# Transposes one merge step later, and w_down copied to bf16 in DRAM during the first merge, in a hybrid decoder layer on eight cores

## The chip, the cores and the metric

The kernel runs on all 8 cores of one Trainium2 chip. Each core computes 4 of the 32 sequences; the cores share no data. The metric is the device time of the slowest core in microseconds (us).

## The reference

One decoder layer on x of 32 sequences, 2048 tokens, 1024 channels, in float32. Two token mixers (A: sliding-window attention with sinks; B: compressed, selected and windowed attention) give `oa` and `ob`. What follows them is what the change touches:

```python
y = gm[:, :, 0] * (oa @ w_proj_a) + gm[:, :, 1] * (ob @ w_proj_b)   # gm = sigmoid(x @ w_gm)
m = y @ w_out
h = layer_norm(ALPHA * x + m, ln1_g, ln1_b)
f = (silu(h @ w_gate) * (h @ w_up)) @ w_down                        # w_down: 2816 x 1024
x = layer_norm(ALPHA * h + f, ln2_g, ln2_b)
```

## The kernel before, in words

Every core goes through its four sequences one after the other (`sequence`): projections (`phase_p`), attention (`attention`), and `phase_cd`, which holds the merge, the gate/up product and the down product. All matmuls are bf16 into float32 PSUM. The weights come as float32. In the first sequence `load` fetches a weight block with a DMA on GpSimd's queue ("pool") that casts it to bf16 into SBUF, and a store on SP's queue writes the bf16 block to a tensor in DRAM (`wg_b`, `wu_b`, `wd_b` and others); four such stores are kept back in a list (`flush_stores(4)`). In the later sequences the same `load` reads the bf16 block from DRAM on SP's queue.

The order of the work is that of the code, written by hand; each engine executes its own instructions in that order, and `Sched` puts semaphore waits in front of an instruction by the buffers it reads and writes.

The merge (`phase_cd`, first loop) goes over 4 token chunks `tc` of 512 tokens and 8 channel blocks `fc` of 128. A block `c1(fc, tc)` is, for each of the two mixers, 8 gate matmuls (`wgm`, L315) and 4 projection matmuls (`Wpa`/`Wpb`, L314) into PSUM banks 0 to 3, a sigmoid on ScalarE (`sg`, L340) that reads bank 0 or 2, a product on VectorE (`tm`), and at the end a sum into `yT`. From the second chunk on, one step of a list `todo` follows each block. The steps handle tiles `t` of 128 tokens:

- `c2_mm(t)`: 16 matmuls with `Wout` (L316) into banks 4 and 5, the residual sum on VectorE (L355), then `ln_front`: statistics on VectorE, a `pow` on GpSimd, one more VectorE operation.
- `c2_norm(t)`: the normalisation on ScalarE (`pre`, L340), and a multiply with `ln1g` on GpSimd.
- `c2_back(t)`: the addition of `ln1b` on VectorE, the cast into `hbf` on ScalarE (L364), the store of `hs` and the load of a new `pre` tile on SP's queue.
- `c2_tr(t)`: 8 transposes of `hbf` on TensorE (L335) into bank 6 or 7, and the copy into `hT` on ScalarE (L364).

24 of the 34 steps stand in the merge; the other ten follow the first ten hidden blocks of the gate/up stage. That stage takes the tokens in two halves. For each of the 22 hidden blocks `hc` it makes 32 matmuls (L317) from `hT` and two ring blocks `ffr` (w_gate, w_up) into banks 0 to 3; a ring of 6 blocks is refilled by `load_ring`, of which four loads are made early, in the merge at `tc == 2`. ScalarE applies Silu (`sgt`, L340), VectorE multiplies (`actf`). In the first half the 22 blocks of `Wd` are loaded too, one at each of the first ten `hc`, two at each of the next six. The down product (L318) follows each half.

Of the kernel before, what the change touches and what calls it, by code (L numbers as in the profile page):

```python
# [6 lines left out]
BF16 = mybir.dt.bfloat16  # L7
# [5 lines left out]
NT = 16  # L13
DH = 64
FFN = 2816
NHC = 22
# [272 lines left out]
class KB:  # L289
# [163 lines left out]
    def load(self, dst, nm, i, b):  # L453

        if nm not in self.wb:
            self.wb[nm] = self.nc.dram_tensor(nm + "_b", list(self.dr[nm].shape), BF16, kind="Internal").ap()
            self.b_wb[nm] = {}

        def part(ap):
            return ap if i is None else ap[:, i, :] if nm == "wd" else ap[i]  # L460

        if any(p[2] is b for p in self.stores):
            self.flush_stores()
        kept = self.b_wb[nm].get(i)
        if kept is not None and kept.w:
            self.s.dma("sp", (dst, part(self.wb[nm])), reads=[kept], writes=[b])
            return
        kept = self.b_wb[nm][i] = Buf(nm)
        self.s.dma("pool", (dst, part(self.dr[nm])), writes=[b])
        self.stores.append((part(self.wb[nm]), dst, b, kept))  # L470
        self.flush_stores(4)

    def flush_stores(self, n=0):
        while len(self.stores) > n:
            out, src, b, kept = self.stores.pop(0)
            self.s.dma("sp", (out, src), reads=[b], writes=[kept])
# [635 lines left out]
    def phase_cd(self, sq):  # L1112
# [36 lines left out]
        def c1(fc, tc):  # L1149
            ts_ = slice(tc * 512, (tc + 1) * 512)  # L1150
            for i in range(2):
                j = self.wgm_at[2 * fc + i]
                for k in range(8):
                    self.mm("c1g", bk[2 * i][:], wgm[:, j, k, :], self.xT[:, k, ts_], k == 0, k == 7,
                            [self.b_wgm[j], b_xT[tc]], [bb[2 * i]])
                Wp = (Wpa, Wpb)[i]
                for k in range(4):
                    self.mm("c1p", bk[2 * i + 1][:], Wp[:, k, fc * 128:(fc + 1) * 128], self.OT[:, 4 * i + k, ts_],
                            k == 0, k == 3, [b_wp[i], self.b_OT[2 * i + k // 2][tc]], [bb[2 * i + 1]])
                self.act(sg[i], bk[2 * i][:], AF.Sigmoid, [bb[2 * i]], [b_sg[i]])  # L1160
                self.tt(tm[i], bk[2 * i + 1][:], sg[i], ALU.mult, [bb[2 * i + 1], b_sg[i]], [b_tm[i]])
            self.tt(yT[tc % 2][:, fc, :], tm[0], tm[1], ALU.add, [b_tm[0], b_tm[1]], [b_yT[tc % 2]])
# [36 lines left out]

        todo = []  # L1200
        for t in range(NT):
            todo.append([(c2_mm, t)] + ([(c2_back, t - 1)] if t else []))
            todo.append([(c2_norm, t)] + ([(c2_tr, t - 1)] if t else []))
        todo += [[(c2_back, NT - 1)], [(c2_tr, NT - 1)]]

        def c2_step():
            for f, t in todo.pop(0):
                f(t)
# [7 lines left out]
        def load_ring(n):  # L1216
            nonlocal nb
            for _ in range(n):
                if nb < len(blocks):
                    nm, hc = blocks[nb]  # L1220
                    self.load(ring[nb % 6][:], nm, hc, b_ring[nb % 6])
                    nb += 1

        for tc in range(4):
            if tc == 2:
                load_ring(4)
            for fc in range(8):
                c1(fc, tc)
                if tc > 0:
                    c2_step()  # L1230
# [21 lines left out]
        for half in range(2):  # L1252
            b_act = [Buf("act%d%d" % (half, i), spans=strided(M_ACT + 1024 * i, 2048, NHC, 1024)) for i in range(2)]
            for hc in range(NHC):
                w = [((half * NHC + hc) * 2 + i) % 6 for i in range(2)]
                load_ring(2)
                for t2 in range(2):
                    tc = 2 * half + t2
# [122 lines left out]
```

How the kernel before makes its waits and increments, by code:

```python
    def _wait(self, e, key, val):  # L89
        if val <= 0:
            return
        if self.seen[e].get(key, 0) >= val:
            return
        self.eng[e].wait_ge(self.sem[key], val)
        self.seen[e][key] = val
# [31 lines left out]
    def op(self, e, fn, reads=(), writes=(), war=(), parts=128):  # L127
        self._deps(e, reads, writes, war)
        if e == "pool":
            if parts != self.pool_parts or parts == 32:
                self._wait(e, e, self.cnt[e])
            self.pool_parts = parts
        inst = fn()
        self.cnt[e] += 1
        c = self.cnt[e]
        inst.then_inc(self.sem[e], 1)
        for b in reads:
            if b.r.get(e, 0) < c:
                b.r[e] = c
        for b in writes:
            b.w = {e: c}
            b.r = {}
        self.n_inst += 1
        return inst
# [1 line left out]
    def dma(self, q, pairs, reads=(), writes=(), war=()):  # L146
        if not isinstance(pairs, list):
            pairs = [pairs]
        keys = self.dma_keys[q]
        key = keys[self.dma_next[q] % len(keys)]
        self.dma_next[q] += 1
        self._wait(q, key, self.dma_val[key])
        self._deps(q, reads, writes, war)
        for out, in_ in pairs:
            self.eng[q].dma_start(out=out, in_=in_).then_inc(self.sem[key], 16)
        self.dma_val[key] += 16 * len(pairs)
        v = self.dma_val[key]
        for b in reads:
            b.r[key] = v
        for b in writes:
            b.w = {key: v}
            b.r = {}
        self.n_inst += len(pairs)
```

## Time and profile before

| | |
|---|---|
| median of 3 runs | 4913.55 us (4782.35 to 5346.75) |
| the profiled execution: its time | 4829.63 us |
| its span, slowest core (6) | 4828.6 us |
| TensorE (PE) busy | 4343.9 us, 90% of the span |
| VectorE (DVE) busy | 2002.6 us, 41% |
| ScalarE (ACT) busy | 1746.8 us, 36% |
| GpSimd (POOL) busy | 989.6 us, 20% |
| DMA | 438.16 MB, mean 91 GB/s |

Busy time is that of the instructions of one engine; matmuls are pipelined, so a matmul record is longer than the time until the next one may start. The granted clock is TensorE's, as a share of full speed. A wait names the engine and tile that released it. Line numbers are those of the code above; helpers that record an operation (`act` L340, `tt` L344, `stt` L355, `cp` L364, `dma` L156, `tr` L335) give their line to all of their callers, so the tile names tell them apart.

### The profile page before, as it was taken

The page shows a single profiled execution, that of the slowest core. Times are in us where ns is not written, and L with a number is a line of the kernel's source. Part 1 is how long each engine was busy: PE and PEld are TensorE (multiplying, and loading weights), DVE is VectorE, ACT ScalarE, POOL GpSimd, SP SyncE. Part 2 cuts the span into 40 slices and gives each one's busy share as a digit, 9 for nine tenths or more (in the row PEclk, how much of TensorE's full clock was granted, in tenths as well). Part 3 has the DMA queues.
Part 4 walks back from the last instruction along what each step waited for, and adds up shares of the span by engine and source line. Part 5 has one row for each costly group of instructions (what it writes and reads, how often), then busy time and mean ns, then how long its engine had stood idle before and what let it go on. Part 6 is the DMA issues. An engine that isn't in the chain of part 4 may idle for free.

```text
span 4828.6 us, 81987 instructions; the slowest of 8 cores (4763.4 to 4828.6 us)
## 1 busy us (share of the span) xinstructions
PE 4343.9 (90%) x26552; PEld 2127.8 (44%) x27000; DVE 2002.6 (41%) x4784; ACT 1746.8 (36%) x2187; POOL 989.6 (20%) x891
## 2 busy tenths in 40 slices
PE   6868899899987899999998789999998788999998
PEld 3434444344444444444444444444444444444443
DVE  2544454132465445422355444523136544542313
ACT  1368433111237843311125872321122685331111
POOL 4321122120342112101143111202024210210101
PEclk8999999999999999999999999999999999999887
DMA  8340236934232012335333002252432201124130
GB/s 146 125 105 2 56 103 151 230 95 127 82 98 66 2 62 79 121 124 140 83 100 126 2 24 74 71 171 79 148 95 84 90 2 54 70 96 153 66 92 35
DMA packets 225809, 438.16 MB, mean 91 GB/s; under 512 B 26864, under 2 KB 98928, under 8 KB 222192
## 3 DMA queue, kind: packets, MB, share of 16 engines
q1 hardware_dynamic: 189312, 380.01, 23.7%
q0 software_dynamic: 33008, 50.77, 7.2%
q8 instruction: 227, 3.72, 0.3%
q10 hardware_dynamic: 3072, 2.10, 0.2%
q14 instruction: 190, 1.56, 0.1%
HBM read 352.95 MB, written 124.31 MB: 99 GB/s over the span
## 4 chain that ended last, share of the span: by engine, by line
PE 70%; DMA 11%; ACT 8%; DVE 5%; issue 4%; SPq 1%; POOL 1%; DVEq 0%; POOLq 0%; ACTq 0%
PE bpair L317 24%; PE bpair L318 13%; PE bpair L315 8%; ACT pt L340 6%; DMA qd<-ro 5%; PE bpair L316 5%; PE bpair L307 4%; PE bpair L314 4%; PE bpair L302 3%; DMA qd<-zr 2%; PE bpair L308 2%; PE bpair L312 2%; DMA ffr<-wg 1%; PE bpair L335 1%; PE bpair L309 1%
## 5 line engine op out<-in xcount | busy, mean ns | idle before, releaser
L317 PE MATMUL bpair<-hT,ffr 128*128 128x512 bf16 x5512 | 1259.4, 389 | 28.1 <-DMA ffr<-wg 19.3
L340 ACT ACTIVATE pt<-bpair 128x1024 bf16<-128x1024 f32 (+1 forms) x1016 | 990.8, 1019 | 241.0 <-PE bpair L313 114.9
L317 PEld LDWEIGHTS bpair<-hT,ffr 128*128 128x128 bf16 x5632 | 558.4, 100 | 716.0 <-issue 148.8
L318 PE MATMUL bpair<-Wd,actf 128*128 128x512 bf16 x2756 | 635.4, 393 | 3.6
L344 DVE TENSOR_TENSOR actf<-sgt,bpair 128x512 bf16<-128x512 f32 x352 | 240.8, 688 | 950.6 <-PE bpair L317 928.5
L340 ACT ACTIVATE sgt<-bpair 128x512 f32<-128x512 f32 x352 | 207.9, 596 | 867.4 <-PE bpair L317 866.9
L302 PE MATMUL bpair<-xT,w 128*128 128x512 bf16 x1615 | 396.2, 398 | 101.2 <-DVE small L344 59.7
L315 PE MATMUL bpair<-xT,wgm 128*128 128x512 bf16 x1996 | 482.7, 382 | 3.5 <-issue 0.4
L318 PEld LDWEIGHTS bpair<-Wd,actf 128*128 128x128 bf16 x2816 | 282.8, 100 | 355.6 <-issue 100.4
L307 PE MATMUL bpair<-Qr,Ksl 128*128 128x512 bf16 x1088 | 341.6, 384 | 77.7 <-ACT pt L340 48.1
L344 POOL TENSOR_TENSOR sb_lnst<-sb_lnst,sb_mhalf 128x1 f32<-128x1 f32 x128 | 70.3, 549 | 1562.6 <-DVE sb_lnst L350 1562.6
L344 POOL TENSOR_TENSOR ro<-t,t 128x512 bf16<-128x512 f32 (+1 forms) x192 | 241.5, 1275 | 372.2 <-DVE small L344 181.7
L344 DVE TENSOR_TENSOR tm<-bpair,sg 128x512 f32<-128x512 f32 x256 | 172.9, 690 | 322.5 <-PE bpair L314 147.0
L315 PEld LDWEIGHTS bpair<-xT,wgm 128*128 128x128 bf16 x2048 | 198.4, 98 | 236.4 <-issue 6.9
L340 ACT ACTIVATE H<-H,sb_lnst 128x1024 f32<-128x1024 f32 x64 | 79.4, 1241 | 610.3 <-DVE sb_lnst L351 610.3
L302 PEld LDWEIGHTS bpair<-xT,w 128*128 128x128 bf16 x1664 | 163.2, 101 | 297.1 <-issue 136.3
L312 PEld LDWEIGHTS bpair<-V,pt 128*128 128x128 bf16 x4352 | 214.6, 98 | 147.0 <-issue 20.7
L364 ACT CAST hbf<-pre 128x1024 bf16<-128x1024 f32 x64 | 66.8, 1044 | 549.2 <-DVE pre L344 549.2
L312 PE MATMUL bpair<-V,pt 128*128 128x65 bf16 x4352 | 237.2, 195 | 10.9 <-DVE tmpo L344 8.4
L340 ACT ACTIVATE sg<-bpair 128x512 f32<-128x512 f32 x256 | 148.3, 597 | 245.7 <-PE bpair L315 235.0
L316 PE MATMUL bpair<-Wout,yT 128*128 128x512 bf16 x1012 | 230.9, 380 | 0.6
L344 POOL TENSOR_TENSOR pre<-pre,ln1g 128x1024 f32<-128x1024 f32 x64 | 164.4, 2568 | 290.9 <-ACT pre L340 290.9
(131 smaller groups left out, 4520.7 us busy)
## 6 DMA issues: line engine op xcount, KB each, us to landing
ffr<-wg_b SPq DMA_DIRECT2D x154, 256.0 KB, 3.1
ffr<-wu_b SPq DMA_DIRECT2D x154, 256.0 KB, 3.1
pre<-x SPq DMA_DIRECT2D x64, 512.0 KB, 3.5
hs<-pre SPq DMA_DIRECT2D x64, 512.0 KB, 2.6
H<-hs SPq DMA_DIRECT2D x64, 512.0 KB, 3.9
out<-H SPq DMA_DIRECT2D x64, 512.0 KB, 2.6
Wd<-wd_b SPq DMA_DIRECT2D x66, 256.0 KB, 4.4
xT<-xt POOLq DMA_DIRECT2D x16, 1024.0 KB, 15.2
```

What stands on the lines that cost most here:

```text
L302: "fm": lambda *a, **k: t.matmul(*a, **k),
L307: "ss": lambda *a, **k: t.matmul(*a, **k),
L308: "sw": lambda *a, **k: t.matmul(*a, **k),
L312: "pvs": lambda *a, **k: t.matmul(*a, **k),
L314: "c1p": lambda *a, **k: t.matmul(*a, **k),
L315: "c1g": lambda *a, **k: t.matmul(*a, **k),
L316: "c2": lambda *a, **k: t.matmul(*a, **k),
L317: "gu": lambda *a, **k: t.matmul(*a, **k),
L318: "dn": lambda *a, **k: t.matmul(*a, **k),
L340: return self.s.op("act", lambda: nc.scalar.activation(out=out, in_=in_, func=func, **kw), reads, writes, war)
L344: return self.s.op(eng, lambda: e.tensor_tensor(out=out, in0=in0, in1=in1, op=op), reads, writes, war, out.shape[0])
L364: return self.s.op("act", lambda: nc.scalar.copy(out=out, in_=in_), reads, writes, war)
```

## The change

Two edits. In the list of steps the transposes of tile t-2 stand now behind `c2_mm(t)` and `c2_back(t-1)`, where those of tile t-1 stood behind `c2_norm(t)`. And w_down is copied block by block from float32 to bf16 within DRAM, by casting DMAs on GpSimd's queue, one ahead of each of the first 22 blocks `c1` of the first sequence; the loads of `Wd` in the first sequence then find the bf16 block kept and run on SP's queue, as in the later sequences, and their stores fall away.

```diff
+    def copy_wd(self, i):
+
+        if not i:
+            self.wb["wd"] = self.nc.dram_tensor("wd_b", list(self.dr["wd"].shape), BF16, kind="Internal").ap()
+            self.b_wb["wd"] = {}
+        b = self.b_wb["wd"][i] = Buf("wd")
+        self.s.dma("pool", (self.wb["wd"][:, i, :], self.dr["wd"][:, i, :]), writes=[b])
...
         for t in range(NT):
-            todo.append([(c2_mm, t)] + ([(c2_back, t - 1)] if t else []))
-            todo.append([(c2_norm, t)] + ([(c2_tr, t - 1)] if t else []))
-        todo += [[(c2_back, NT - 1)], [(c2_tr, NT - 1)]]
+            todo.append([(c2_mm, t)] + ([(c2_back, t - 1)] if t else []) + ([(c2_tr, t - 2)] if t > 1 else []))
+            todo.append([(c2_norm, t)])
+        todo += [[(c2_back, NT - 1), (c2_tr, NT - 2)], [(c2_tr, NT - 1)]]
...
             for fc in range(8):
+                i = 8 * tc + fc
+                if i < NHC and "wd" not in self.wb or i and len(self.b_wb["wd"]) == i < NHC:
+                    self.copy_wd(i)
                 c1(fc, tc)
```

ScalarE in the first merge, before (`sg` the sigmoids of a block, `pre` the normalisation, `hbf` the cast, `hT` the copy of the transposes):

```order
379 L364 CAST hbf_79_7786<-pre_75_7782 128x1024
380 L340 ACTIVATE sg_68_7775<-bpair 128x512
381 L340 ACTIVATE sg_69_7776<-bpair 128x512
382 L340 ACTIVATE pre_76_7783<-pre_76_7783,sb_lnst 128x1024
383 L364 COPY hT_44<-bpair 128x8x128
384 L340 ACTIVATE sg_68_7775<-bpair 128x512
385 L340 ACTIVATE sg_69_7776<-bpair 128x512
```

The same place after:

```order
378 L364 CAST hbf_79_7786<-pre_75_7782 128x1024
379 L364 COPY hT_44<-bpair 128x8x128
380 L340 ACTIVATE sg_68_7775<-bpair 128x512
381 L340 ACTIVATE sg_69_7776<-bpair 128x512
382 L340 ACTIVATE pre_76_7783<-pre_76_7783,sb_lnst 128x1024
383 L340 ACTIVATE sg_68_7775<-bpair 128x512
384 L340 ACTIVATE sg_69_7776<-bpair 128x512
```

The copy into `hT` has moved from behind the normalisation to directly behind the cast, ahead of the two sigmoids of the next block.

TensorE at the same place, before (`wgm` gate matmuls, `OT,Wpa`/`Wpb` projections, `Wout` those of `c2_mm`, `hbf` the transposes):

```order
1023 L316 MATMUL bpair<-Wout_7746,yT_72_7779 128x512 x16
1024 L315 MATMUL bpair<-xT_43,wgm_2818 128x512 x8
1025 L314 MATMUL bpair<-OT_125,Wpa_2819 128x512 x4
1026 L315 MATMUL bpair<-xT_43,wgm_2818 128x512 x8
1027 L314 MATMUL bpair<-OT_125,Wpb_2820 128x512 x4
1028 L335 MATMUL bpair<-sb_ident,hbf_79_7786 128x128 x8
1029 L315 MATMUL bpair<-xT_43,wgm_2818 128x512 x8
```

and after:

```order
1032 L316 MATMUL bpair<-Wout_7746,yT_72_7779 128x512 x16
1033 L335 MATMUL bpair<-sb_ident,hbf_79_7786 128x128 x8
1034 L315 MATMUL bpair<-xT_43,wgm_2818 128x512 x8
1035 L314 MATMUL bpair<-OT_125,Wpa_2819 128x512 x4
1036 L315 MATMUL bpair<-xT_43,wgm_2818 128x512 x8
1037 L314 MATMUL bpair<-OT_125,Wpb_2820 128x512 x4
1038 L315 MATMUL bpair<-xT_43,wgm_2818 128x512 x8
```

The transposes stand directly behind the 16 matmuls of `c2_mm`, one block earlier in the row than before but for an older tile.

GpSimd in the first sequence's gate/up stage, before (`ffr` the ring, `sb_lnst` the pow, `pre` the multiply):

```order
187 L344 TENSOR_TENSOR sb_lnst<-sb_lnst,sb_mhalf 128x1
188 L156 DMA Wd_9935<-wd 128x1024
189 L156 DMA ffr_82_7797<-wg 128x1024
190 L156 DMA ffr_83_7798<-wu 128x1024
191 L344 TENSOR_TENSOR pre_74_7781<-pre_74_7781,ln1g_7767 128x1024
192 L156 DMA Wd_9935<-wd 128x1024
```

and after, first at the start of the merge, then in that stage:

```order
155 L156 DMA wgm_2818<-wgm 128x1024 x4
156 L156 DMA Wout_7746<-wout 128x8192
157 L156 DMA wd_b<-wd 128x1024 x9
158 L344 TENSOR_TENSOR sb_lnst<-sb_lnst,sb_mhalf 128x1
159 L156 DMA wd_b<-wd 128x1024
...
201 L344 TENSOR_TENSOR sb_lnst<-sb_lnst,sb_mhalf 128x1
202 L156 DMA ffr_82_7797<-wg 128x1024
203 L156 DMA ffr_83_7798<-wu 128x1024
204 L344 TENSOR_TENSOR pre_74_7781<-pre_74_7781,ln1g_7767 128x1024
```

The casting transfers of `wd` have left the stage and stand in the merge, nine of them behind the load of Wout with nothing of GpSimd's between them.

## Rows read from the trace of the kernel before

**Rows 1.** Cores: span, granted clock; then the medians of the dies.
```profile
core 6: 4828.6 us, clock 0.964
...
die 0 (median of its cores): 4765.8 us, clock 0.980
die 1 (median of its cores): 4800.8 us, clock 0.967
```

**Rows 2.** Windows: start:end, length; PE, PEld, DVE, ACT, POOL busy; PEclk, DMA share, GB/s.
```profile
535.00:763.00 228.00, 213.75 (x1019) 97.89 (x1038) 116.20 (x189) 67.94 (x95) 39.76 (x31) 0.99 0.33 93
763.00:964.00 201.00, 178.56 (x800) 78.53 (x817) 50.23 (x79) 44.03 (x64) 47.26 (x71) 0.95 0.98 215
1958.00:2126.00 168.00, 167.16 (x798) 77.49 (x812) 50.22 (x79) 43.61 (x63) 14.23 (x9) 1.00 0.49 159
...
4541.00:4723.00 182.00, 180.80 (x692) 76.06 (x704) 34.50 (x51) 27.39 (x45) 2.90 (x2) 0.83 0.28 87
```

**Rows 3.** Tile ffr, first gate/up stage of two sequences: ns min/median/max, first and last start.
```profile
L317 PEld LDWEIGHTS bpair<-hT,ffr x704: 94/98/153, 763.8 to 963.8; 128*128 128x128 bf16 x176
...
L317 PEld LDWEIGHTS bpair<-hT,ffr x704: 96/98/98, 1958.2 to 2125.8; 128*128 128x128 bf16 x176
```

**Rows 4.** Waits in 763 to 964 us, PE and SP's queue: total, times, longest.
```profile
PE bpair L317 <- DMA ffr<-wg: 19.3, 8, 4.8
...
SPq L94 <- DMA Wd<-wd: 46.6, 18, 4.8
```

**Rows 5.** Waits of PE over the whole span.
```profile
PE bpair L335 <- ACT hbf L364: 53.6, 44, 1.5
```

**Rows 6.** Timeline of one merge cycle, second sequence: start, length, engine, operation, idle.
```profile
1825.83 1.89 PE L315 MATMUL bpair<-xT,wgm 128*128 128x512 bf16 x8
...
1829.88 1.22 DVE L344 TENSOR_TENSOR pre<-pre,ln1b 128x1024 f32<-128x1024 f32 x1
...
1831.19 1.04 ACT L364 CAST hbf<-pre 128x1024 bf16<-128x1024 f32 x1 [8.71 <-DVE pre L344]
1832.14 1.08 ACT L340 ACTIVATE sg<-bpair 128x512 f32<-128x512 f32 x2
...
1832.38 0.61 PE L335 MATMUL bpair<-sb_ident,hbf 128*128 128x128 bf16 x8 [1.20 <-ACT hbf L364]
...
1832.87 1.89 PE L315 MATMUL bpair<-xT,wgm 128*128 128x512 bf16 x8
...
1834.24 1.01 ACT L364 COPY hT<-bpair 128x1024 bf16<-128x1024 bf16 x1
...
1835.13 0.61 ACT L340 ACTIVATE sg<-bpair 128x512 f32<-128x512 f32 x1
...
1838.05 3.19 PE L316 MATMUL bpair<-Wout,yT 128*128 128x512 bf16 x13
```

**Rows 7.** Timeline of a step in the second sequence's gate/up stage.
```profile
1986.35 7.07 PE L317 MATMUL bpair<-hT,ffr 128*128 128x512 bf16 x31
...
1991.71 1.04 ACT L364 CAST hbf<-pre 128x1024 bf16<-128x1024 f32 x1 [9.57 <-DVE pre L344]
...
1992.66 1.08 ACT L340 ACTIVATE sgt<-bpair 128x512 f32<-128x512 f32 x2
...
1993.70 2.54 PE L317 MATMUL bpair<-hT,ffr 128*128 128x512 bf16 x11
```

**Rows 8.** DMA issues: count, KB each, median us to landing; last, GpSimd's issue time in ns.
```profile
ffr<-wg POOLq DMA_DIRECT2D x22, 256.0 KB, 12.9
...
Wd<-wd_b SPq DMA_DIRECT2D x66, 256.0 KB, 4.4
...
Wd<-wd POOLq DMA_DIRECT2D x22, 256.0 KB, 16.1
wd_b<-Wd SPq DMA_DIRECT2D x22, 256.0 KB, 11.7
...
L156 POOL DMA_DIRECT2D Wd<-wd x22: 527/547/591, 778.2 to 911.9; - x22
```

## Prediction

> **What bounds the kernel now.** I read the cores first. Core 6 is the slowest, 4828.6 us at a granted clock of 0.964; the median of die 0 is 4765.8 us at 0.980 [rows 1]. So 62.8 us of the profiled time belong to die 1 alone. The windows show where: in the last gate/up stage of the last sequence the clock stands at 0.83, where the undisturbed stages stand at 0.99 or 1.00 [rows 2]. Nothing in the change touches that, but it tells how far a measured time can lie from the sum.
>
> Second, the same windows say which engine bounds the two stages that the change touches. In the merge of the first sequence TensorE is busy 213.75 of 228 us, while DMA is at a share of 0.33. In the first gate/up stage of the second sequence it is busy 167.16 of 168 us with DMA at 0.49. In the same stage of the first sequence, where the weights still come in as float32 and are written back as bf16, DMA is at 0.98 of all 16 engines over 201 us, and the clock at 0.95 [rows 2]. Third, the tile view of the ring weights gives that stage's length from its first to its last weight load: 200.0 us in the first sequence (763.8 to 963.8), 167.6 us in the second (1958.2 to 2125.8) [rows 3]. The first sequence thus pays 32.4 us for its transfers. The wait view puts 19.3 us of it down to one kind of load, and SP's queue stands 46.6 us behind landings of Wd blocks [rows 4]; the rest of the 32.4 us is small waits in the records and the lower clock.
>
> Fourth, TensorE's waits over the span: the transposes of the merged tiles waited 44 times for ScalarE's cast `hbf`, 53.6 us in total, so 11 times per sequence and 1.2 us each [rows 5].
>
> **Part one: the transposes, one merge step later.** What is removed is clear: tile t-2 was cast two `c1` blocks and a `c2_mm` earlier, so these 44 waits go. What comes in their place is read from the timeline of one cycle (two steps) in the second sequence [rows 6]. Take as zero the first matmul behind `c2_mm`, 1825.83. VectorE's chain for tile t ends in `ln_back` of t-1 at 1829.88; the cast starts at 1831.19, the two sigmoids behind it at 1832.14; the transposes start at 1832.38 after a wait of 1.20 us, and the next block's gate matmuls at 1832.87, which is 7.04 us after zero. These matmuls write bank 0, which the first of those two sigmoids reads. So they have a second condition, hidden now: sigmoid start 1832.14, plus 0.60 us, plus the 0.15 us from the end of the cast (1832.23) to the transposes, makes 1832.89. It ties with the transposes. Take the wait on the cast away and PE stands at the same moment at the sigmoid.
>
> The change makes it worse. ScalarE is served in program order, and its copy into `hT` moved along with the transposes: it stood behind the norm, in the step in which ScalarE had room, and stands now between the cast and the two sigmoids. One copy moves the next sigmoid by 1835.13 - 1834.24 = 0.89 us [rows 6]. So the first sigmoid starts at 1833.03, and the gate matmuls at 1833.03 + 0.60 + 0.15 = 1833.78, that is 0.91 us later than now. TensorE itself would be ready at 1825.83 + 0.46 (transposes) + 5.18 (the block, 1832.87 to 1838.05) = 1831.47, so it waits 2.31 us for ScalarE. The vector chain hangs on `c2_mm` alone and nothing of it moves, so this repeats in each cycle. The first cycle that has a `c2_back` (t = 1) has no copy yet and costs nothing new; t = 2 to 11 are ten cycles, 9.1 us a merge.
>
> Four more such steps (t = 12 to 15) lie in the gate/up stage [rows 7]. There zero is 1986.35, the cast 1991.71, the Silu into `sgt` 1992.66, and the next block but one begins at 1993.70 with no wait. With the copy in between, sgt starts at 1993.55 and frees the bank at 1994.30: 0.6 us each. One set of eight transposes (0.46 us) also moves from the merge into this stage. That is 2.9 us, with the merge 12.0 us a sequence, 48 us in four. The bounds: -53.6 us if all waits go and nothing follows; +48 plus the chance that the later copies hold up a second sigmoid, which I see no row for. I take +48, since each term is a duration in rows 6 and 7.
>
> **Part two: wd copied to bf16 during the first merge.** Removed from the first gate/up stage: 22 casting loads on GpSimd's queue (median 16.1 us to landing) and 22 stores on SP's (11.7 us). Added there: 22 plain loads on SP's queue, which the later sequences do in 4.4 us [rows 8]. Added in the merge: 22 copies on GpSimd's queue, nine of them at once behind the load of Wout, the rest one per block; GpSimd is busy 39.76 of 228 us there [rows 2], and each issue costs it about 0.55 us [rows 8] between two of its small operations, so no pow and no multiply waits for it.
>
> The DMA work by the windows: first sequence 0.98 x 201 = 197 us of all 16 engines, second 0.49 x 168 = 82 us. The 115 us between them are what 40 ring blocks (44 less the four that `load_ring(4)` fetches in the merge) and 22 Wd blocks, 62 in all, cost more by being cast and stored, 1.85 us a block. Taking 22 of these away leaves 197 - 41 = 156 us of work in a stage that is 167.6 + 2.9 = 170.5 us long, a share of 0.92. It fits, closely. So I expect the 32.4 us back but for some 2 to 3 us of remaining waits: -30 us. Bounds: 0 if the ring stays late, -32.4 if nothing is left. The 41 us go into the merge, whose share rises from 0.33 to about 0.5; copies from DRAM to DRAM have no row, the nearest are these casting blocks, and even at twice their price the share stays near 0.7. Below, the copies could cost nothing at all. No wait on them shows: the first Wd load comes 200 us later. SP's queue has one danger: it now issues the stores of the ring one block later than before (with four kept back and two, not three, coming per block), behind `hs` stores that wait for VectorE; a ring slot can't be loaded again before that.
>
> The profile of before gives these loads a landing time of 12.9 us at the median [rows 8]. The Trainium skill ("DMA: Bandwidth & Descriptors", "Anatomy of one DMA") fits a transfer from GpSimd as 2.0 us and bytes over 436 GB/s, some 3 us for a block of 512 KB. By that estimate 62 blocks move in 75 us, the queue would never be full, the 32.4 us would have another cause and part two would bring nothing: the sum would be the second rival's. The row of 0.98 speaks against it.
>
> **Sum.** +48 - 30 = +18 us on 4829.6 us, the profiled execution (4828.6 us of span and 1 us around it): 4848 us. That is 66 us under the median of the runs shown, 4913.55, and 65 over their lowest, 4782.35; the 18 us are the prediction, and the clock of die 1 sets the rest.
>
> **Rivals.**
> First, nothing takes the place of the wait: if bank 0 is free in time (the sigmoid served earlier than I read, or the copy shorter behind a cast), the 53.6 us go and part two brings 32.4: 4744 us, 1.8% faster, not slower. For it stands the row of 44 waits; against it the tie of 1832.87 and 1832.89. It decides from the point at which the first sigmoid starts less than 4.9 us behind `c2_mm`, and it starts at 6.3. 10%.
> Second, part two brings nothing: the ring is still late because its stores are issued later, and a share of 0.92 is near full. Then only part one counts: 4829.6 + 48 = 4878 us, 1.0% slower. For it stands the closeness of 0.92; against it that the second sequence keeps TensorE busy through the stage with Wd loads on the same queue. 15%.
> Third, the copy costs nothing but the wait stays as a wait on the sigmoid: +0 - 30, 4800 us. 13%.
>
> **How the numbers follow.** My forecast holds 62%. A measurement of this kernel tells about 2% from no change, 98 us here, and none of the four cases reaches it; what is left over is the clock. Faster by over 2% takes die 1 undisturbed and the first rival, 3%. Slower by over 2% takes a disturbance like that of rows 1 on top of the second rival, 5%. Within 2%: 92%. The range reaches down to 4786, my sum without die 1's 62.8 us, and some way to the first rival, 4770; up to the runs' own median plus 18, 4931, of which I leave the edge: 4920.
>
> **What would show it.** The wait of the transposes on `hbf` is gone, and in its place TensorE's gate matmuls wait for the sigmoid about 40 times, 2.3 us each. A merge is 9 us longer, the second sequence's gate/up stage about 170.5 instead of 167.6 us, the first one's 170 to 174 instead of 200. The DMA share there is near 0.9, and 0.5 in the first merge. If merges are shorter than now I have read the order on ScalarE wrongly; if the first gate/up stage stays at 190 us or more, the ring's round trip and not the amount of traffic was the bound.

## Result, and the profile after

| | before | after |
|---|---|---|
| median of the timed runs | 4848.8 us (4 runs, 4782.35 to 5346.75) | 5029.07 us (4 runs, 4824.9 to 5319.69) |
| profiled execution | 4829.63 us | 4825.37 us |
| ratio | | 1.0088, 95% interval 1.0044 to 1.0131 |

The change makes the kernel slower by 0.9%, some 42 us of 4782. The medians and the two profiled executions can't be compared, since in two runs of each kernel, and at the end of the profiled one of before (the 0.83 of [rows 2]), a die stood at a lower clock for a long stretch; the ratio, and the cores of die 0 in every profile used below, are free of it. The cores of the changed kernel, beside [rows 1]:

```profile
core 5: 4824.3 us, clock 0.975
...
die 0 (median of its cores): 4814.1 us, clock 0.976
die 1 (median of its cores): 4822.0 us, clock 0.975
```

Die 0 went from 4765.8 to 4814.1 us, and its clock from 0.980 to 0.976.

The waits of TensorE over the span answer [rows 5]:

```profile
PE bpair L315 <- ACT sg L340: 86.4, 40, 2.5
```

The 44 waits on the cast (53.6 us) are gone. In their place TensorE's gate matmuls (L315) wait 40 times for the sigmoid, 2.16 us each; four more of 2.2 us (one per sequence, where the gate/up stage begins) stand under L317. One cycle in the timeline of the second sequence, as [rows 6]:

```profile
1849.69 1.46 PE L315 MATMUL bpair<-xT,wgm 128*128 128x512 bf16 x6
...
1852.87 1.22 DVE L344 TENSOR_TENSOR pre<-pre,ln1b 128x1024 f32<-128x1024 f32 x1
...
1854.17 1.04 ACT L364 CAST hbf<-pre 128x1024 bf16<-128x1024 f32 x1 [8.71 <-DVE pre L344]
...
1855.12 1.01 ACT L364 COPY hT<-bpair 128x1024 bf16<-128x1024 bf16 x1
1856.03 1.09 ACT L340 ACTIVATE sg<-bpair 128x512 f32<-128x512 f32 x2
...
1856.77 1.89 PE L315 MATMUL bpair<-xT,wgm 128*128 128x512 bf16 x8 [2.17 <-ACT sg L340]
```

The cast starts at 1854.17, the copy 0.95 us later, the sigmoids another 0.91 us later, and the matmuls stand 2.17 us until the first of these has read bank 0. From the cast to those matmuls it is 2.60 us; in [rows 6] it was 1832.87 - 1831.19 = 1.68 us.

The windows of core 5, each one stage (merge and gate/up stage of the first sequence, the same of the second, the merge of the third), as [rows 2]:

```profile
544.00:785.00 241.00, 217.21 (x1040) 98.40 (x1038) 116.05 (x189) 69.97 (x97) 50.36 (x52) 0.98 0.52 114
785.00:966.00 181.00, 171.22 (x816) 77.27 (x815) 50.09 (x79) 43.30 (x62) 35.83 (x49) 0.99 0.87 206
1732.00:1977.00 245.00, 220.91 (x1042) 99.42 (x1041) 116.49 (x190) 70.11 (x98) 35.58 (x23) 0.97 0.22 73
1977.00:2147.00 170.00, 168.23 (x814) 77.16 (x813) 49.95 (x79) 43.16 (x62) 14.22 (x9) 1.00 0.55 155
2915.00:3157.00 242.00, 218.57 (x1044) 99.11 (x1045) 116.52 (x190) 70.15 (x98) 35.59 (x23) 0.98 0.21 75
```

A merge lasts 241 to 245 us here, the first gate/up stage 181 instead of 201 us at a DMA share of 0.87 (before 0.98), the second 170. The first merge carries the copies at a share of 0.52 and is no longer than the others. What stands new beside the waits is the clock column: 0.97 and 0.98 in the merges.

For the comparison of all kernels I took the four cores of die 0 and four sequences each: a stage lasts from its first matmul to the first of the next stage. "Lost to the clock" is the sum of (1 - granted clock) x time over a merge.

| kernel | merge, us (median of 16) | lost to the clock | merge without it | first gate/up stage | later ones |
|---|---|---|---|---|---|
| before | 229.4 | 1.7 | 227.8 | 197.9 to 200.3 | 167.8 |
| after | 242.3 | 5.1 (3.4 to 6.8) | 237.1 | 177.3 to 178.8 | 170.7 to 172.5 |

Four merges are 4 x 12.9 = 52 us longer, three later gate/up stages some 11 us, and the first one 21 us shorter: +42 us. (The medians of die 0 lie 48 us apart; the other 6 us lie outside these stages.)

### The profile page after: what moved, and what is told of

Its sections match the earlier page's. It is cut to its first block, busy times and chain, and to the rows that moved or that the text cites. A ratio compares the mean times of both kernels' runs of the same rounds, so it can differ in the third digit from the quotient of the medians.

```text
span 4824.3 us, 82367 instructions; the slowest of 8 cores (4800.3 to 4824.3 us)
## 1 busy us (share of the span) xinstructions
PE 4321.7 (90%) x27000; PEld 2115.7 (44%) x27000; DVE 2002.5 (42%) x4784; ACT 1753.3 (36%) x2187; POOL 989.4 (21%) x891
## 4 chain that ended last, share of the span: by engine, by line
PE 70%; DMA 10%; ACT 8%; issue 5%; DVE 4%; SPq 1%; POOL 1%; DVEq 0%; ACTq 0%; POOLq 0%
PE bpair L317 24%; PE bpair L318 13%; PE bpair L315 9%; ACT pt L340 6%; DMA qd<-ro 5%; PE bpair L316 5%; PE bpair L307 4%; PE bpair L314 4%; PE bpair L302 4%; DMA qd<-zr 2%; PE bpair L308 2%; PE bpair L309 2%; PE bpair L312 1%; SPq L156 1%; ACT hT L364 1%
## 5 line engine op out<-in xcount | busy, mean ns | idle before, releaser
L317 PE MATMUL bpair<-hT,ffr 128*128 128x512 bf16 x5632 | 1229.3, 380 | 23.9 <-ACT sg L340 8.7
L317 PEld LDWEIGHTS bpair<-hT,ffr 128*128 128x128 bf16 x5632 | 549.2, 98 | 692.7 <-issue 43.2
L318 PE MATMUL bpair<-Wd,actf 128*128 128x512 bf16 x2816 | 609.1, 379 | 0.0
L315 PE MATMUL bpair<-xT,wgm 128*128 128x512 bf16 x2048 | 504.0, 391 | 86.4 <-ACT sg L340 86.4
L315 PEld LDWEIGHTS bpair<-xT,wgm 128*128 128x128 bf16 x2048 | 199.9, 100 | 338.9 <-issue 126.0
```

The costliest lines, as they stand in the source:

```text
L315: "c1g": lambda *a, **k: t.matmul(*a, **k),
L317: "gu": lambda *a, **k: t.matmul(*a, **k),
L318: "dn": lambda *a, **k: t.matmul(*a, **k),
```

## Experiments

Times in the tables are medians or ranges over die 0 as above.

### Each part alone

`e1_transposes_only` is the kernel before with the new list of steps alone; `e2_wd_copy_only` has the old list and `copy_wd`.

```diff
--- e2_wd_copy_only against the changed kernel
-            todo.append([(c2_mm, t)] + ([(c2_back, t - 1)] if t else []) + ([(c2_tr, t - 2)] if t > 1 else []))
-            todo.append([(c2_norm, t)])
-        todo += [[(c2_back, NT - 1), (c2_tr, NT - 2)], [(c2_tr, NT - 1)]]
+            todo.append([(c2_mm, t)] + ([(c2_back, t - 1)] if t else []))
+            todo.append([(c2_norm, t)] + ([(c2_tr, t - 1)] if t else []))
+        todo += [[(c2_back, NT - 1)], [(c2_tr, NT - 1)]]
```

> The kernel before with only the transposes moved one step later; Wd is loaded and stored in the first sequence as before. Theory (ScalarE's copy into hT stands between the cast and the first sigmoid, TensorE waits about 2.2 us for bank 0 in 11 cycles of each merge, and the granted clock falls in the merges on top): all four merges last 240 to 245 us (before 228 to 231), gate/up stages of sequences two to four 170.7 to 172.5 us, the first one stays near 200; ratio to before about 1.013 to 1.015. Rival (the copies within DRAM or their issue on GpSimd lengthen the merge): the first merge is back near 229 us, and the others too if something lingers; ratio near 1.00.

> The kernel before with only w_down copied block by block in DRAM. Theory: merges as before, 228 to 231 us, the first one too, with 11 waits of 1.2 us on the cast; the first gate/up stage 174 to 178 us instead of 198 to 201; ratio 0.995. Rival (the copies cost time in the first merge): the first merge several us longer than the other three.

| kernel | merge | lost to the clock | without it | first gate/up stage | later ones |
|---|---|---|---|---|---|
| e1_transposes_only | 243.6 | 6.8 | 236.9 | 200.4 to 203.7 | 170.7 to 172.7 |
| e2_wd_copy_only | 229.6 | 1.7 | 228.1 | 173.2 to 178.1 | 167.8 |

e1 took 4851.6 and 4852.0 us beside one run of before of 4787.6 on the same chip: 1.0134. TensorE's waits in e1 (core 1) and in e2 (core 2):

```profile
PE bpair L315 <- ACT sg L340: 85.6, 40, 2.5
```

```profile
PE bpair L335 <- ACT hbf L364: 54.5, 44, 1.6
```

Both came as expected in the main, and the parts add up. The transposes bring all of the loss and the lower clock: summed over the stages and averaged over die 0, e1 is 67 us longer than before, 17 us of it lost to the clock. The copies bring all of the gain, 23 us in the first gate/up stage, and cost the merge nothing (the first merge of e2 is 229.5 to 229.8 us, as before). The rival, that the copies lengthen the merge, falls. The ratio of e2 as a whole stays open; its stages on die 0 are clear.

### Is it the place of the copy on ScalarE?

`e3_copy_behind_sigmoids` leaves transposes and cast where the change has them and moves only ScalarE's copy:

```diff
+        def c2_cp(t):
+            tbi = 6 + t % 2 if t < 12 else 6
+            tb = bk[tbi][:].bitcast(BF16)
             self.cp(hT[:, :, t * 128:(t + 1) * 128], tb.rearrange("p (a b) -> p a b", b=128), [bb[tbi]],
                     [b_hT[t // 4]], eng="act")
...
-            todo.append([(c2_norm, t)])
+            todo.append([(c2_norm, t)] + ([(c2_cp, t - 2)] if t > 1 else []))
```

> Both parts of the change, but ScalarE's copy into hT is a function of its own and stands one step after the transposes, behind the normalisation. Theory: the first sigmoid starts again 6.3 us behind c2_mm, TensorE waits 1.4 us for it instead of 2.2 in 11 cycles a merge, a cycle is as long as before (15.6 us) and not 16.5; merges 228 to 231 us, clock loss as before; ratio to before 0.995. Rival for the extra 4 to 5 us a merge (the clock falls because the transposes stand directly behind c2_mm, not because of the length of the wait): the clock in the merges stays at 0.97 to 0.98 and the merges at 232 us or more.

`e8_second_copy` does the opposite, the copy is executed twice:

```diff
+            for _ in range(2):
+                self.cp(hT[:, :, t * 128:(t + 1) * 128], tb.rearrange("p (a b) -> p a b", b=128), [bb[tbi]],
+                        [b_hT[t // 4]], eng="act")
```

> The changed kernel with ScalarE's copy into hT executed twice (the same values), to measure the mechanism. Theory: the first sigmoid is 0.9 us later still, TensorE's wait on sg grows from 2.2 to 3.1 us in ten cycles a merge, merges 9 us longer than those of the changed kernel without the clock (246 us), and the clock in the merges lower again or as low, 248 to 256 us in all; gate/up stages two to four 174 us and more. Rival (something other than ScalarE's order sets the wait): the wait stays at 2.2 us.

TensorE's waits in e3 and in e8, core 2 of each:

```profile
PE bpair L315 <- ACT sg L340: 53.5, 40, 1.8
```

```profile
PE bpair L315 <- ACT sg L340: 126.0, 40, 3.6
```

The wait is 1.34 us at the mean with no copy between cast and sigmoid, 2.16 with one, 3.15 with two. (The first such wait of a merge, whose step has no transposes yet, is 1.7 us in all three kernels; most of the others are 1.25, 2.17 and 3.27 us.) The second merge of core 2 in the windows, for before, after, e3 and e8:

```profile
1733.00:1961.00 228.00, 214.31 (x1047) 98.00 (x1048) 116.19 (x189) 68.60 (x97) 35.64 (x23) 1.00 0.21 79
```

```profile
1731.00:1973.00 242.00, 216.91 (x1021) 98.90 (x1042) 116.19 (x189) 69.61 (x97) 35.61 (x23) 0.98 0.21 75
```

```profile
1711.00:1941.00 230.00, 214.21 (x1023) 98.08 (x1043) 116.53 (x190) 68.24 (x97) 35.62 (x23) 0.99 0.22 78
```

```profile
1756.00:2012.00 256.00, 220.00 (x1021) 99.53 (x1042) 116.23 (x189) 79.49 (x106) 35.61 (x23) 0.97 0.19 71
```

| kernel | mean wait per cycle | merge | lost to the clock (least to most) | without it | later gate/up |
|---|---|---|---|---|---|
| before | 1.22 (on the cast) | 229.4 | 1.7 (0 to 3.0) | 227.8 | 167.8 |
| e3 | 1.34 | 229.8 | 1.7 (0 to 1.7) | 228.1 | 168.5 |
| after | 2.16 | 242.3 | 5.1 (3.4 to 6.8) | 237.1 | 170.7 to 172.5 |
| e8 | 3.15 | 264.2 | 18.8 (6.6 to 33.0) | 245.6 | 175.2 to 177.9 |

Two things follow. Each copy between cast and sigmoid costs a merge 9 us (228.1, 237.1, 245.6), as the timeline said. And the clock follows the length of the wait. The 1.7 us of before aren't the price of its waits: `e4` below has none of them and loses the same, in one stretch at the lower level of 1.2 GHz where a merge begins. Past the first 5 us of a merge, the traces of die 0 (16 merges each) show no stretch at that level in before, e2 and e3, with waits of 1.2 or 1.3 us once in some 16 us, and none in e4. They show 38 in the changed kernel and 42 in e1, with waits of 2.2 us, two or three a merge, and 96 in e8, three to nine a merge. In front of every one of these TensorE had just stood in such a wait. e8 was timed on another chip than e3, but e5 to e7 below, from the chip of e8, show none.

e3 has the transposes where the changed kernel has them and loses nothing, so their place isn't the cause; e1 loses at least as much as the changed kernel, without the copies in DRAM. e3 whole: 4761.1 and 4766.3 us beside 4787.6, 0.995, of which all is part two. e8 took 4984.5 us in its one run. The forecasts for e3 held. That for e8 held for the wait and for the merge without the clock (246, measured 245.6), but not for the clock: 248 to 256 us were expected and 254.7 to 274.9 measured, so the price of a longer wait in clock was set too low a second time.

### A version that beats both

`e4_back_one_step_later` moves the addition, the cast and their DMAs one step later too (steps of the list `todo`), so that ScalarE's row has the copy right behind the transposes and the cast behind the normalisation:

```diff
-            todo.append([(c2_mm, t)] + ([(c2_back, t - 1)] if t else []) + ([(c2_tr, t - 2)] if t > 1 else []))
-            todo.append([(c2_norm, t)])
+            todo.append([(c2_mm, t)] + ([(c2_tr, t - 2)] if t > 1 else []))
+            todo.append([(c2_norm, t)] + ([(c2_back, t - 1)] if t else []))
```

> Both parts, and c2_back (the addition, the cast, the store of hs, the load of pre) one step later too, so that the cast stands behind the normalisation and the copy behind c2_mm. Theory: neither the cast nor the copy stands ahead of a sigmoid that TensorE waits for; no waits on sg or hbf in the merges, merges of 214 to 216 us at a clock of 1.00, gate/up stages two to four 168.3 us; in all 56 us less for the merges and 22 to 25 for the first gate/up stage, ratio 0.983. Rival (ScalarE or VectorE is too full and another wait takes its place, on tm or yT): merges of 224 us or more.

It took 4688.2, 4692.2 and 4695.6 us beside 4787.6 for before: 0.980, some 95 us. Merges 213.2 us (211.5 without the clock), later gate/up stages 168.4 us; no wait on `sg` or `hbf` stands among TensorE's waits. Of the stages on die 0, four merges bring 65 us and the first gate/up stage, by part two, 22. A cycle of it on core 0:

```profile
1843.79 2.67 POOL L344 TENSOR_TENSOR pre<-pre,ln1g 128x1024 f32<-128x1024 f32 x1 [2.31 <-ACT pre L340]
...
1844.16 3.38 DVE L344 TENSOR_TENSOR pre<-pre,ln1b 128x1024 f32<-128x1024 f32 x1
...
1847.60 3.62 PE L316 MATMUL bpair<-Wout,yT 128*128 128x512 bf16 x16
...
1847.62 1.04 ACT L364 CAST hbf<-pre 128x1024 bf16<-128x1024 f32 x1 [3.98 <-DVE pre L344]
1848.58 1.08 ACT L340 ACTIVATE sg<-bpair 128x512 f32<-128x512 f32 x2
...
1851.05 0.61 PE L335 MATMUL bpair<-sb_ident,hbf 128*128 128x128 bf16 x8
...
1851.50 1.89 PE L315 MATMUL bpair<-xT,wgm 128*128 128x512 bf16 x8
1851.75 1.01 ACT L364 COPY hT<-bpair 128x1024 bf16<-128x1024 bf16 x1 [2.10 <-PE bpair L335]
```

The cast and the sigmoids behind it run while TensorE is busy with `c2_mm`, and the gate matmuls at 1851.50 find bank 0 read since 1849.18. The prediction of 214 to 216 us was 1 to 3 us too high.

### What is left of the first gate/up stage

Part two alone (e2) brought 23 us of the 32, not 30; that leaves some 8 us over a later stage, and 6 to 7 in the changed kernel. The critical chain of the changed kernel (core 5) in this stage: start, length, what.

```profile
866.23 1.23 DVE pre L344
867.52 0.32 SPq L156
868.08 0.32 SPq L156
...
868.87 0.91 SPq L156
869.93 11.12 DMA wu_b<-ffr
...
881.64 8.96 DMA ffr<-wu
```

A ring store stands in SP's queue behind the store of `hs`, which waits for VectorE; then it takes 11.12 us, and the slot's next load another 8.96. TensorE waits five times for ring loads in this stage, 7.8 us in all. The same stage of this core in windows, at its start and late in it:

```profile
785.00:800.00 15.00, 15.00 (x76) 6.98 (x75) 7.00 (x13) 3.85 (x5) 4.89 (x5) 1.00 0.61 141
...
880.00:900.00 20.00, 19.07 (x89) 8.54 (x88) 3.62 (x6) 3.35 (x6) 3.69 (x7) 1.00 1.04 231
900.00:920.00 20.00, 17.06 (x79) 7.34 (x77) 3.94 (x6) 2.98 (x5) 2.64 (x5) 1.00 1.03 277
```

The DMA share (second number from the end) goes from 0.61 to 1.04. So both could be it, the late store (theory A) or the full engines (theory B). Three variants of e4:

```diff
--- e5_keep_two_stores
-        self.flush_stores(4)
+        self.flush_stores(2 if nm in ("wg", "wu") else 4)
--- e6_wd_one_per_block
-                    for i in ([hc] if hc < 10 else [2 * hc - 10, 2 * hc - 9] if hc < 16 else []):
+                    for i in [hc]:
--- e7_all_copied_in_attention
+        if "wd" not in self.wb:
+            for i in range(NHC):
+                for nm in ("wg", "wu", "wd"):
+                    self.later.append(lambda nm=nm, i=i: self.copy_block(nm, i))
+                    self.later += [lambda: None] * 2
```

> The kernel e4 with two, not four, stores of ring blocks kept back, so that SP's queue issues each one block earlier. Theory A (after the change the first gate/up stage is 175 to 178 us because the ring's stores come one block too late for the slot): it falls to 169 to 171 us. Theory B (it is late because all 16 DMA engines are full in its second half, where two Wd blocks come per hidden block): no change, 174 to 178 us.

> The kernel e4 with one Wd block loaded at each of the 22 hidden blocks instead of two at blocks 10 to 15. Theory B (the peak of DMA traffic): the peak goes, but the stores and H loads behind it stay; the first gate/up stage falls by 2 to 4 us, to 171 to 174 us. Theory A: no change. All other stages as in e4.

> The kernel e4 with w_down, w_gate and w_up all copied to bf16 in DRAM, block by block, during the first sequence's attention, where the DMA share is 0.1 or less; the first gate/up stage then loads plain bf16 blocks without stores, as the other sequences do. Theory: that stage lasts 168.4 us as in the others, the 8 us or so that part two left go; attention is not longer, since a copy takes 1.85 us of DMA and one is issued every 2 to 3 us. Ratio to before 0.980, 0.002 under e4. Rival (GpSimd, which adds the attention outputs, is held up by the 66 issues and their waits for a free semaphore): the first attention grows by 5 us or more and nothing is gained.

| kernel | first gate/up stage | the same stage for the second half of the tokens | DMA share late in the first (core 0) |
|---|---|---|---|
| e4 | 174.7 to 179.8 | 151.9 | 1.00 |
| e5 | 171.0 to 173.4 | 152.6 to 160.6 | |
| e6 | 170.1 to 173.6 | 151.9 | 1.02 |
| e7 | 170.7 to 173.0 | 151.9 | 0.55 |

The windows behind the last column, e4, e6 and e7, and last the changed kernel's core 0 at the same place:

```profile
870.00:930.00 60.00, 55.15 (x243) 23.97 (x241) 10.32 (x15) 8.79 (x16) 6.33 (x12) 0.94 1.00 250
```

```profile
865.00:925.00 60.00, 60.00 (x278) 26.96 (x277) 12.38 (x18) 10.15 (x17) 6.89 (x13) 1.00 1.02 253
```

```profile
870.00:930.00 60.00, 60.00 (x280) 27.20 (x279) 12.39 (x18) 10.15 (x17) 0.00 (x0) 1.00 0.55 179
```

```profile
900.00:960.00 60.00, 60.00 (x280) 27.18 (x279) 12.37 (x18) 10.15 (x17) 7.39 (x14) 1.00 1.04 271
```

Neither theory holds whole. Stores issued earlier (e5) take 4 to 5 us off the stage, where A said 169 to 171 us and B no change, but the time comes back in the second half. There the last two ring stores stand in SP's queue behind a store of `out` that waits for VectorE, and the load of the same slot stands behind them; TensorE waits 5.81 us for it. Wd loads spread over all 22 blocks (e6) take off 5 to 6 us, about as B said, and nothing comes back. But late in that stage the engines are as full as ever (1.02) and TensorE is busy all 60.00 us, as it is in the changed kernel on core 0 at 1.04. So a share of 1 by itself costs nothing here; what costs is a single ring load that lands late. Why it lands earlier in e6 wasn't tested apart.

With all weights copied during attention (e7) the share late in the stage is 0.55 and TensorE still waits once, 2.69 us on core 0 and 6.00 us on core 4, for a ring load on SP's queue; where the clock stayed up and the wait was short the stage took 170.7 us. My forecast of 168.4 us missed by about 3 us. The trace of core 0 shows what held that load up. The kernel's `flush_stores()` in front of the stage has four stores left, three of `wgm` and one of `Wout`, which stand in SP's queue right ahead of it (767.14 to 768.67). The load is issued at 769.26, 10.4 us into the stage, and lands after 9.94 us. In the second sequence, which has no such stores, the load at the same place is issued 8.3 us into the stage and lands after 5.0 us, without a wait. In the 11 us from the load on the DMA share is 0.99 in the first sequence and 0.53 in the second. Attention, from its first matmul to the merge's, lasted 284 to 294 us on the cores of die 0 (before 284 to 289), so it hardly grew. Whole, e5 took 4698.1 us and e7 4691.9 and 4699.0 us, no better than e4 as far as these runs tell; the ratio of e6 stays open.

## Why the prediction was right and wrong

The mechanism of part one was right, and so were its durations. Foretold were about 40 waits on the sigmoid of 2.3 us, measured 44 of 2.16 (those under L317 counted); a merge 9.1 us longer, measured 9.3 without the clock (227.8 to 237.1); the later gate/up stages 170.5 us, measured 170.7 where the clock stayed up. The rule by which it was found, that ScalarE's copy had moved between the cast and a sigmoid that TensorE needs, is shown by e3 and e8, which take the copy out and add one.

What failed are two terms of the sum. I forecast +18 us; measured was about +42 (ratio 1.0088).

- The clock, a term put at nothing. "+48, since each term is a duration in rows 6 and 7" left out that longer waits lower the granted clock. At the mean of die 0 the four merges lost 21 us to it instead of 6, and the three later gate/up stages 3 instead of none: 18 us. The prediction put the clock down to the die alone ("Nothing in the change touches that"). That was the wrong step: a wait grown from 1.2 to 2.2 us did touch it.
- Part two, "-30 us". With part one's 2.9 us the forecast for the first gate/up stage was -27; measured was -21 (e2, part two alone: -23 instead of -30). Part of the difference is the ring's store behind `hs` in SP's queue, the danger that I named and priced at nothing: e5, which issues the stores earlier, takes 4 to 5 us off the stage. Part is where the Wd loads stand (e6, 5 to 6 us). The share of 0.92 worked out for the stage came out as 0.87, but as a mean over it: 0.61 at its start and above 1.0 from 880 to 940. A mean share didn't say whether each block lands in time.

With these, 18 (the forecast) + 18 + 6 = 42. The sum itself holds a small slip: the eight transposes that move into the gate/up stage were added there (0.46 us) and not taken off the merge, 1.8 us in four sequences. And the lower end, my sum without die 1's 62.8 us, is 4785, not 4786.

The median of the runs, 5029 us, lies outside the range; the two lower runs, 4825 us each, lie in it. "Within 2%", at 92%, came true, and so did the direction, at more than twice the size.

The first rival (all waits go, 4744 us) fell: the second condition behind the first was there. The third expects what e3 shows, 0.995: the wait stands on the sigmoid, 1.34 us, and the gain of part two is left; but the changed kernel isn't that kernel. The second (part two brings nothing) fell with the 21 us. The estimate from the Trainium skill ("DMA: Bandwidth & Descriptors", "Anatomy of one DMA") would have had the 32.4 us come from something else than transfers. The traces disagree with it here: the blocks landed after 12.9 us at the median and not after some 3 [rows 8], and the stage shrank by 21 us when transfers were taken out of it.

## What to carry to other kernels

When a wait is taken away, look for the second condition that ends at the same moment, and at what else the moved step issues: here a 1 us copy on ScalarE, moved along with eight transposes, stood in front of the operation that freed the next bank. An operation that depends on a late result (the cast) belongs at the end of an engine's row for the step, behind everything that TensorE will ask for soon; moving it (e4) made each merge 16 us shorter. Where a change lengthens a wait of TensorE, its price is the wait and what the clock loses by it; here that was 37 us and 15 us in the merges. And a mean DMA share doesn't tell whether loads come in time. Stretches at 1.02 and 1.04 cost nothing, and in e7, whose stage as a whole was far from full, one load still came late; ask of each load what stands ahead of it in its queue.

## What the runs showed of the hardware that I had not expected

- Short, regular waits of TensorE can bring its granted clock down. With waits of 2.2 us once per cycle of 16 us it fell to its lower level two or three times in each merge, past the merge's first 5 us (38 times in 16 merges), and the merges lost 5.1 us to the clock at the median; with 3.3 us it fell 96 times and they lost 18.8 us, up to 33.0. With waits of 1.2 to 1.3 us it never fell there; the 1.7 us that those merges lost stand at their beginning and are the same in e4, which has no such waits.
- In e4 VectorE's addition of `ln1b` took 3.38 us where it had taken 1.22 [rows 6]. It began at 1844.16 and ran while GpSimd multiplied another tile (`pre<-pre,ln1g`, 2.67 us from 1843.79). On core 0 the 58 additions of e4 that overlap such a multiply have a median of 3.37 us, the 6 others 1.22, and GpSimd's multiply stays at 2.6 to 2.7. It was hidden there; VectorE's busy time rose from 2002.6 to 2122.0 us over the span.
